# Expert blocks of 32 rows on four column groups, plain float32 weights in four whole buffers, loads begun while planning

## The chip, the cores and the metric

The kernel runs on one core of a Trainium2 chip. The metric is the device time of one launch in microseconds, the median of the timed runs. Everything is float32, and one launch does the whole of the computation below.

## What is computed

The reference is a trunk of two layers over 1,280 tokens of width 1,024 (256 context tokens and 1,024 latent tokens). Layer 0 mixes tokens by a convolution module, layer 1 by a gated linear attention. Each is followed by a mixture of experts. Layer 0's works on all 1,280 tokens, layer 1's on the 1,024 latent ones. The change concerns the mixture of experts alone:

```python
g_idx = argmax(h @ wg + bg)                      # one of 4 groups
inner = (h @ wr + br).reshape(t, 4, 8)[:, g_idx] # 8 experts in it
top_v, top_i = top_k(inner, 2)                   # two experts a token
top_w = softmax(top_v) * g_prob[g_idx]
expert = g_idx * 8 + top_i
# for each token's two experts e:
y = (silu(x @ w1[e]) * (x @ w3[e])) @ w2[e]      # w1, w3: 1024x512, w2: 512x1024
out[token] += top_w * y
```

Each layer has 32 experts with 6.29 MB of weights each. Layer 0 has 2,560 pairs of a token and an expert, layer 1 has 2,048. How many rows an expert gets depends on the data.

## The kernel before

The program is a row of stages; each is one block in which all engines run their own instruction streams, and a stage begins when all engines have finished the one ahead. In each layer the order around the experts is: `conv_out` or `gla_output` (which writes the normalised rows `hd` to memory and leaves the router's scores `lg` in a tile), `route`, `experts`, then `combine_values` or `combine`. `conv_taps` is an earlier stage of layer 0.

**`route`** plans. VectorE picks the two experts of each token, TensorE counts rows with two products (L1042, L1043), and VectorE works out each row's rank in its expert, in which block of rows it stands (`first`) and at which place in it (`mine`). From tables of places and blocks (`in_slot`, `in_blk`) TensorE makes the list of tokens of each block (L1048), `plan.token`. It also makes `plan.block`, the expert of each block, and `plan.fresh`, whether a block has another expert than the one ahead. VectorE waits for the constant tables at the start. The blocks are 128 rows long, and an expert takes as many as it needs; experts with no more than 128 rows take one.

**`experts`** runs one block after another. GpSimd gathers the block's 128 rows from `hd` into `xg` (L1317), after TensorE has turned the block ahead. TensorE turns them (`moe_pxt`, L1349), ScalarE and VectorE split them into a high part in float32r and the rest (`moe_xt_hi`, `moe_xt_lo`). The weights are split in the same way when a block is fresh: ScalarE copies each half matrix of 1 MB to `hi` (L1408) and VectorE subtracts it to get `lo` (L1479). Each product is three products, high by high, high by low and low by high:

```python
def product3(pe, out, xh, xl, wh, wl, start, stop):
    pe.matmul(out, xh, wh, start=start, stop=False)
    pe.matmul(out, xh, wl, start=False, stop=False)
    return pe.matmul(out, xl, wh, start=False, stop=stop)
```

In a block TensorE runs w1's and w3's products (24 matmuls of 512 columns each), turns the rows of the block behind it in order, runs w2's product of the block ahead (24 matmuls), and turns its own block's `a` = silu times product (`moe_pat`, L1388). ScalarE takes `py` out to `y` (L1418) and stores it (L1422). SyncE loads weights into `raw` (L1282): w1 and w3 have two raw buffers, w2 has one; a load waits until VectorE has made the low part of what stood there. At the end of layer 0 SyncE writes zeros over the blocks that are not used (L1302).

The bodies stand twice in a loop with a test whether the block is in the count. What is read from a table (`value_load`) sets which branch is taken.

## Time and profile before

| | |
|---|---|
| median of 3 runs | 3072.42 us |
| lowest, highest | 3071.2, 3075.68 us |
| the profiled execution's own time | 3072.33 us |
| its span, first to last instruction | 3070.6 us |
| mean granted clock of TensorE, share of full | 0.899 |
| TensorE busy (matmul / weight load) | 2519.3 / 2033.0 us |
| VectorE, ScalarE, GpSimd busy | 2006.1, 1432.9, 331.4 us |
| moved by DMA | 689 MB, 224 GB/s over the span |

Busy times of TensorE are lengths of pipelined instructions; two can overlap, so how densely they follow is read from their starts. In a row, `output<-inputs` names the tiles, and what stands in square brackets is the engine's idle time ahead of the group with what ended it. The rows on which the prediction rests stand in a section of their own below.

### The profile page before, as it was taken

The page shows a single profiled execution, that of the slowest core. Times are in us where ns is not written, and L with a number is a line of the kernel's source. Part 1 is how long each engine was busy: PE and PEld are TensorE (multiplying, and loading weights), DVE is VectorE, ACT ScalarE, POOL GpSimd, SP SyncE. Part 2 cuts the span into 40 slices and gives each one's busy share as a digit, 9 for nine tenths or more (in the row PEclk, how much of TensorE's full clock was granted, in tenths as well). Part 3 has the DMA queues.
Part 4 walks back from the last instruction along what each step waited for, and adds up shares of the span by engine and source line. Part 5 has one row for each costly group of instructions (what it writes and reads, how often), then busy time and mean ns, then how long its engine had stood idle before and what let it go on. Part 6 is the DMA issues. An engine that isn't in the chain of part 4 may idle for free. (4 is left out here: it accounts for less than half of the span.)

```text
span 3070.6 us, 40694 instructions
## 1 busy us (share of the span) xinstructions
PE 2519.3 (82%) x13249; PEld 2033.0 (66%) x13249; DVE 2006.1 (65%) x1989; ACT 1432.9 (47%) x1596; POOL 331.4 (11%) x381
## 2 busy tenths in 40 slices
PE   4488773695799999999948998979693999999970
PEld 0467662584588888888836876768583788888850
DVE  1559999665657786588526402347565788888855
ACT  0311001452546676577424313458331777777742
POOL 0000000100001000100012100043100100010004
PEclk8589887797799999999978999989796999999985
DMA  9354341221878899799655411025551999999956
GB/s 306 119 166 140 127 159 70 99 103 65 291 261 306 323 331 357 264 360 389 247 182 202 143 52 46 14 78 171 205 191 61 375 389 385 389 388 394 394 211 227
DMA packets 294341, 689.13 MB, mean 224 GB/s; under 512 B 22764, under 2 KB 49588, under 8 KB 294222
## 3 DMA queue, kind: packets, MB, share of 16 engines
q1 hardware_dynamic: 263058, 584.81, 52.8%
q0 software_dynamic: 17472, 56.72, 5.6%
q10 hardware_dynamic: 13712, 46.30, 4.0%
q8 instruction: 61, 1.00, 0.1%
q14 instruction: 38, 0.31, 0.0%
HBM read 597.74 MB, written 91.06 MB: 224 GB/s over the span
## 5 line engine op out<-in xcount | busy, mean ns | idle before, releaser
L1479 DVE TENSOR_TENSOR moe_w_lo<-moe_w_raw,moe_w_hi 128x2048 fp32r<-128x2048 f32 x384 | 861.8, 2285 | 81.8 <-ACT moe_w_hi L1408 48.0
L1408 ACT ACTIVATE moe_w_hi<-moe_w_raw 128x2048 fp32r<-128x2048 f32 x384 | 713.8, 1908 | 59.1 <-issue 38.3
L99 PE MATMUL moe_pg<-moe_w_hi,moe_xt_hi 128*128 128x512 f32 x592 | 243.4, 411 | 11.3 <-DVE moe_xt_lo L1490 5.9
L99 PE MATMUL moe_py<-moe_w_hi,moe_at_hi 128*128 128x512 f32 x592 | 242.0, 409 | 11.9 <-DVE moe_w_lo L1479 8.2
L100 PE MATMUL moe_pg<-moe_w_lo,moe_xt_hi 128*128 128x512 f32 x592 | 236.6, 400 | 0.0
L101 PE MATMUL moe_pg<-moe_w_hi,moe_xt_lo 128*128 128x512 f32 x592 | 236.1, 399 | 0.0
L100 PE MATMUL moe_py<-moe_w_lo,moe_at_hi 128*128 128x512 f32 x592 | 235.4, 398 | 0.0
L101 PE MATMUL moe_py<-moe_w_hi,moe_at_lo 128*128 128x512 f32 x592 | 235.3, 397 | 0.0
L101 PE MATMUL moe_pu<-moe_w_hi,moe_xt_lo 128*128 128x512 f32 x592 | 234.3, 396 | 0.0
L99 PE MATMUL moe_pu<-moe_w_hi,moe_xt_hi 128*128 128x512 f32 x592 | 234.1, 396 | 0.0
L100 PE MATMUL moe_pu<-moe_w_lo,moe_xt_hi 128*128 128x512 f32 x592 | 234.1, 396 | 0.0
L1525 DVE TENSOR_TENSOR moe_a<-moe_sil,moe_pu 128x512 f32<-128x512 f32 x74 | 50.9, 688 | 182.0 <-issue 133.2
L531 ACT ACTIVATE taps_sg<-taps_zg,channel_vectors 128x512 f32<-128x512 f32 (+1 forms) x24 | 14.8, 616 | 285.5 <-PE taps_za L101 285.5
L1418 ACT ACTIVATE moe_y<-moe_py 128x1024 f32<-128x1024 f32 x74 | 76.0, 1027 | 148.8 <-PE moe_py L101 148.8
L1433 ACT ACTIVATE moe_xt_hi<-moe_pxt 128x1024 fp32r<-128x1024 f32 x74 | 75.8, 1025 | 134.5 <-PE moe_pxt L1349 134.5
L99 PEld LDWEIGHTS moe_pg<-moe_w_hi,moe_xt_hi 128*128 128x128 f32 x592 | 113.1, 191 | 36.2 <-issue 12.4
L99 PEld LDWEIGHTS moe_py<-moe_w_hi,moe_at_hi 128*128 128x128 f32 x592 | 112.4, 190 | 35.9 <-issue 12.3
L1311 POOL COPY moe_idx<-plan_token 128x1 int32 (+1 forms) x76 | 16.0, 210 | 1077.1 <-PE moe_pxt L1349 1076.9
L101 PEld LDWEIGHTS moe_pg<-moe_w_hi,moe_xt_lo 128*128 128x128 f32 x592 | 113.0, 191 | 27.4
L101 PEld LDWEIGHTS moe_py<-moe_w_hi,moe_at_lo 128*128 128x128 f32 x592 | 112.2, 190 | 27.1
L99 PE MATMUL cv_acc<-cv_w_hi,ht_next_hi 128*128 128x512 f32 x288 | 116.9, 406 | 14.8 <-DVE ht_next_lo L2038 14.8
L99 PEld LDWEIGHTS moe_pu<-moe_w_hi,moe_xt_hi 128*128 128x128 f32 x592 | 111.2, 188 | 26.9
(348 smaller groups left out, 5397.5 us busy)
## 6 DMA issues: line engine op xcount, KB each, us to landing
moe_w_raw<-in_moe_w SPq DMA_DIRECT2D x384, 1024.0 KB, 12.7
taps_ada_w<-in_ada_w SPq DMA_DIRECT2D x40, 1024.0 KB, 6.9
scratch_experts_out<-moe_y ACTq DMA_DIRECT2D x57, 512.0 KB, 6.4
taps_raw<-in_conv_pw_w SPq DMA_DIRECT2D x20, 512.0 KB, 8.6
scan_v<-scratch_gla_values SPq DMA_DIRECT2D x20, 512.0 KB, 3.6
ada_w<-in_ada_w SPq DMA_DIRECT2D x4, 2048.0 KB, 29.8
cv_raw<-in_gla_w_in SPq DMA_DIRECT2D x16, 512.0 KB, 4.8
scratch_gla_out<-scan_o SPq DMA_DIRECT2D x16, 512.0 KB, 6.4
```

Source lines behind the costliest of these rows:

```text
L99: pe.matmul(out, xh, wh, start=start, stop=False)
L100: pe.matmul(out, xh, wl, start=False, stop=False)
L101: return pe.matmul(out, xl, wh, start=False, stop=stop)
L531: act.activation(sg[g][:, 0:m], zg[g][:, 0:m], ACT.Sigmoid, bias=vecs[:, n, V_BG:V_BG + 1])\
L1311: pool.tensor_copy(idx[:, :], plan.token[:, ds(k, 1)]).then_inc(s("idx_ready"), 1)
L1408: act.activation(hi[m][:, cut, :], raw[m][p][:, cut, :], ACT.Copy).then_inc(s(f"{m}_hi{h}"), 1)
L1418: act.activation(y[:, :], py[:, :], ACT.Copy).then_inc(s("y_out"), 1)
L1433: act.activation(xt_hi[:, :, :], pxt[:, :, :], ACT.Copy).then_inc(s("xt_hi"), 1)
L1479: dve.tensor_tensor(lo[m][:, cut, :], raw[m][p][:, cut, :], hi[m][:, cut, :].bitcast(F32), ALU.subtract).then_inc(s(f"{m}_lo{h}"), 1)
L1525: dve.tensor_tensor(a[:, :], sil[:, :], pu[:, :], ALU.mult).then_inc(s("a_ready"), 1)
```

## The change

- **Blocks are 32 rows.** `route` plans blocks of 32, in a fixed order of the experts (`EXPERT_ORDER`: expert 0 of each group, then expert 1 of each, and so on); each expert has at least one block. `plan.ends` says after which block each expert ends. `plan.fresh`, `plan.taken` and the table behind them go.
- **Four column groups.** In a product of 32 rows the output has 32 partitions. Four of them stand side by side: for w1 and w3 together each strip of 32 partitions takes 128 of the 512 hidden columns of both matrices, for w2 each strip takes 256 of the 1,024 output columns. All tiles of the stage shrink accordingly. A row of `hd` is gathered as four pieces of 256 values, to the four strips.
- **Plain float32.** Weights and rows are not split; each product is one float32 product.
- **Four whole buffers.** `Feed` holds four experts' weights (w1, w3, w2), 6.29 MB each. The loads of expert x + 3 start when expert x - 1 is done. The order is fixed, so SyncE needs no table to know which expert comes.
- **Loads begun while planning.** SyncE issues the loads of three experts in `route`; the planner's own tiles lie in the fourth buffer.
- **The loops.** TensorE goes by experts: the code of one block stands four times with tests, once in a loop for blocks 5 to 16 and once in a loop for more, for each of the four buffers, and that once ahead of the loop over experts and once in it. The other engines go by blocks, four bodies in a loop. GpSimd gathers four blocks ahead.
- **Around it.** The zeros are written in `conv_taps` by one DMA of 4 MB on ScalarE's queue. The planner's first constant (`ranks`) is loaded in the stage ahead. The token list product is cut into four strips.

```diff
-GROUPS, PER_GROUP, EXPERTS, FF, BLK = 4, 8, 32, 512, 128
+GROUPS, PER_GROUP, EXPERTS, FF, BLK = 4, 8, 32, 512, 32
+EXPERT_ORDER = [g * PER_GROUP + e for e in range(PER_GROUP) for g in range(GROUPS)]
+AHEAD_X = 4
+ROUND = float(1 << 23)
...
+                        if g == 2 and n == 1:
+                            act.wait_ge(s("zeros_set"), 1)
+                            act.dma_start(d.yd[2 * TOK:, :].rearrange("(p r) (s n) -> p (r s) n", p=P, n=D // 4),
+                                          zeros[:, :].unsqueeze(1).to_broadcast([P, EXPERTS * BLK // P * 4, D // 4]))\
+                                .then_inc(s("covered"), 16)
                         for at in units_behind(n, g):
...
+    PAIR = 2 * KC * FF
+    WORDS = PAIR + FF // P * D
...
+    def load_pair(self, sp, x):
+        e, b = EXPERT_ORDER[x], x % self.BUFS
+        for m, src in enumerate((self.d.w1, self.d.w3)):
+            for h in range(2):
+                sp.dma_start(self.pair[:, b, m, h * KC // 2:(h + 1) * KC // 2, :].rearrange("p (s c) n -> p s (c n)", c=2),
+                             src[self.layer, e, h * D // 2:(h + 1) * D // 2, :].rearrange("(s p c) n -> p s (c n)", p=P, c=2))\
+                    .then_inc(self.sem(f"pair_loaded{b}"), 16)
+    def load_back(self, sp, x):
+        e, b = EXPERT_ORDER[x], x % self.BUFS
+        for h in range(2):
+            sp.dma_start(self.back[:, b, 2 * h:2 * h + 2, :],
+                         self.d.w2[self.layer, e, h * FF // 2:(h + 1) * FF // 2, :].rearrange("(k p) n -> p k n", p=P))\
+                .then_inc(self.sem(f"back_loaded{b}"), 16)
...
+                for x in range(feed.AHEAD):
+                    feed.load_pair(sp, x)
+                    feed.load_back(sp, x)
...
-                pe.wait_ge(s("hot_slots"), 4)
                 for j in range(2 * nt):
-                    last = pe.matmul(pi[:, :], in_slot[:, j, :], in_blk[:, j, :], start=j == 0, stop=j == 2 * nt - 1)
+                    if j % nt == 0:
+                        pe.wait_ge(s("hot_slots"), 2 * (j // nt + 1))
+                    for r in range(0, P, BLK):
+                        last = pe.matmul(pi[r:r + BLK, :], in_slot[:, j, :], in_blk[:, j, :],
+                                         start=j == 0, stop=j == 2 * nt - 1)
                 last.then_inc(s("slots_done"), 1)
...
+                for x in range(feed.AHEAD, BUFS):
+                    feed.load_pair(sp, x)
+                    feed.load_back(sp, x)
+                for x in range(EXPERTS):
+                    times = x // BUFS + 1
+                    sp.wait_ge(feed.sem(f"pair_loaded{x % BUFS}"), 64 * times)
+                    sp.sem_inc(s("pair_ready"), 1)
+                    sp.wait_ge(feed.sem(f"back_loaded{x % BUFS}"), 32 * times)
+                    sp.sem_inc(s("back_ready"), 1)
+                    if 1 <= x < EXPERTS - feed.AHEAD:
+                        done = sp.value_load(plan.ends[0:1, x - 1:x], min_val=1, max_val=nb)
+                        sp.wait_ge(s("pair_done"), done)
+                        feed.load_pair(sp, x + feed.AHEAD)
+                        sp.wait_ge(s("back_done"), done)
+                        feed.load_back(sp, x + feed.AHEAD)
...
+                def gather(k, p):
+                    pool.tensor_copy(idx[:, p:p + 1], plan.token[:, ds(k, 1)]).then_inc(s("idx_ready"), 1)
+                    pool.wait_ge(s("idx_ready"), k + 1)
                     pool.sem_inc(s("gathers"), 1)
...
+                def out_product(out, buf):
+                    for c in range(STRIPS):
+                        for j in range(STRIPS):
+                            last = pe.matmul(out[j * BLK:(j + 1) * BLK, 0:CUT], at[:, c * BLK:(c + 1) * BLK],
+                                             feed.back[:, buf, c, j * CUT:(j + 1) * CUT], start=c == 0, stop=c == STRIPS - 1)
+                    last.then_inc(s("back_done"), 1)
+                def rows_of(k, x, b, nth):
+                    pe.wait_ge(s("xt_ready"), k + 1)
+                    if nth == 0:
+                        pe.wait_ge(s("pair_ready"), x + 1)
+                    for c in range(KC):
+                        for j in range(STRIPS):
+                            last = pe.matmul(pg[j * BLK:(j + 1) * BLK, 0:2 * P].rearrange("t (m n) -> t m n", m=2),
+                                             xt[:, c % 2, (c // 2) * BLK:(c // 2 + 1) * BLK],
+                                             feed.pair[:, b, :, c, j * P:(j + 1) * P], start=c == 0, stop=c == KC - 1)
+                    last.then_inc(s("pair_done"), 1)
+                    turn_x(k + 1)
+                    if started(k, 1):
+                        pe.wait_ge(s("at_ready"), k)
+                        if nth < 2:
+                            pe.wait_ge(s("back_ready"), x + nth)
+                        pe.wait_ge(s("y_out"), k)
+                        out_product(py, (b - 1) % BUFS if nth == 0 else b)
+                    pe.wait_ge(s("a_ready"), k + 1)
+                    pe.transpose(pat[:, 0:P], a[:, :], ident[:, :]).then_inc(s("at_turned"), 1)
+                def expert(x, b):
+                    first = 0 if isinstance(x, int) and x == 0 else \
+                        pe.value_load(plan.ends[0:1, ds(x - 1, 1)], min_val=1, max_val=nb)
+                    end = pe.value_load(plan.ends[0:1, ds(x, 1)], min_val=1, max_val=nb)
+                    rows_of(first, x, b, 0)
+                    for r in range(1, SOME):
+                        with pe.If(first + r < end):
+                            rows_of(first + r, x, b, r)
+                    with pe.If(first + SOME < end):
+                        with pe.Fori(SOME, MANY) as r:
+                            with pe.If(first + r < end):
+                                rows_of(first + r, x, b, SOME)
+                        with pe.If(first + MANY < end):
+                            with pe.Fori(MANY, (nb - EXPERTS) // 2) as r:
+                                with pe.If(first + r < end):
+                                    rows_of(first + r, x, b, SOME)
+                SOME, MANY = 4, 16
                 pe.wait_ge(s("ident"), 16)
-                turn_x(1)
-                blocks(pe, body, lambda count, last: out_product(count, last, 1))
+                turn_x(0)
+                for b in range(BUFS):
+                    expert(b, b)
+                with pe.Fori(1, EXPERTS // BUFS) as i:
+                    for b in range(BUFS):
+                        expert(i * BUFS + b, b)
+                count = pe.value_load(plan.block[0:1, 0:1], min_val=plan.fewest, max_val=nb)
+                pe.wait_ge(s("at_ready"), count)
+                pe.wait_ge(s("back_ready"), EXPERTS)
+                out_product(py_last, (EXPERTS - 1) % BUFS)
             @block.scalar
...
+                def take_x(k):
+                    act.wait_ge(s("xt_turned"), k + 1)
+                    act.activation(xt[:, :, :], pxt[:, 0:2 * P].rearrange("p (c n) -> p c n", c=2), ACT.Copy)\
+                        .then_inc(s("xt_ready"), 1)
+                def store(k, src, stored):
+                    act.dma_start(d.yd[ds(k * BLK, BLK), :].rearrange("t (s n) -> s t n", n=CUT), src).then_inc(s(stored), 16)
+                def body(k, i, p):
+                    act.wait_ge(s("pair_done"), k + 1)
+                    if started(k, 1):
+                        act.wait_ge(s("a_ready"), k)
+                    act.activation(sil[:, :], pg[:, 0:P], ACT.Silu).then_inc(s("sil_ready"), 1)
+                    take_x(k + 1)
+                    if started(k, 1):
+                        b = (p - 1) % UNROLL
+                        act.wait_ge(s("back_done"), k)
+                        if started(k, UNROLL + 1):
+                            act.wait_ge(s(f"y_stored{b}"), (i - (1 if p == 0 else 0)) * 16)
+                        act.activation(y[b][:, :], py[:, 0:CUT], ACT.Copy).then_inc(s("y_out"), 1)
+                        act.wait_ge(s("y_out"), k + 1)
...
+                def bring_x(k, i, p):
+                    dve.wait_ge(s(f"gathered{p}"), (i + 1) * 16)
+                    if started(k, 1):
+                        dve.wait_ge(s("xt_turned"), k)
+                    dve.tensor_copy(x_rows[:, :], xg[p][:, :]).then_inc(s("x_here"), 1)
+                def body(k, i, p):
+                    bring_x(k + 1, i + (p + 1) // UNROLL, (p + 1) % UNROLL)
+                    dve.wait_ge(s("sil_ready"), k + 1)
+                    if started(k, 1):
+                        dve.wait_ge(s("at_turned"), k)
+                    dve.tensor_tensor(a[:, :], sil[:, :], pg[:, P:2 * P], ALU.mult).then_inc(s("a_ready"), 1)
+                    dve.wait_ge(s("at_turned"), k + 1)
+                    dve.tensor_copy(at[:, :], pat[:, 0:P]).then_inc(s("at_ready"), 1)
```

## Rows read from the trace of the kernel before

**Rows 1.** The page, the span in 40 equal slices.
```profile
PE   4488773695799999999948998979693999999970
...
GB/s 306 119 166 140 127 159 70 99 103 65 291 261 306 323 331 357 264 360 389 247 182 202 143 52 46 14 78 171 205 191 61 375 389 385 389 388 394 394 211 227
```

**Rows 2.** Stage table: window, length, busy (count) by engine, granted clock, DMA share, GB/s.
```profile
726.00:781.00 55.00, 17.15 (x71) 15.03 (x70) 35.58 (x90) 3.82 (x8) 0.01 (x1) 0.51 0.06 23
781.00:1579.00 798.00, 767.90 (x3536) 624.76 (x3536) 529.69 (x318) 487.50 (x361) 72.98 (x88) 0.98 0.84 306
...
2330.00:2368.00 38.00, 9.11 (x36) 8.07 (x36) 28.79 (x83) 1.85 (x4) 0.13 (x1) 0.50 0.02 6
2368.00:2991.00 623.00, 587.97 (x2696) 478.07 (x2696) 506.03 (x288) 451.65 (x321) 61.95 (x68) 0.97 0.98 363
...
2500.00:2900.00 400.00, 400.00 (x1858) 325.97 (x1858) 349.33 (x200) 311.37 (x222) 39.33 (x44) 1.00 1.04 389
```

**Rows 3.** Stage table of tile moe_sil alone: VectorE, ScalarE.
```profile
781.00:1579.00 798.00, 28.87 (x42) 24.42 (x42) 0.98 0.84 306
2368.00:2991.00 623.00, 22.02 (x32) 18.52 (x32) 0.97 0.98 363
```

**Rows 4.** Timeline of TensorE in one block: start, length, instruction, count.
```profile
961.78 0.48 PE L99 MATMUL moe_pg<-moe_w_hi,moe_xt_hi 128*128 128x512 f32 x1
...
973.06 1.03 PE L1349 MATMUL moe_pxt<-moe_ident,moe_xg 128*128 128x128 f32 x8
...
979.52 0.60 PE L1388 MATMUL moe_pat<-moe_ident,moe_a 128*128 128x128 f32 x4
```

**Rows 5.** Timeline at a modulation group; that tile's instruction row.
```profile
167.61 0.39 PE L101 MATMUL taps_za<-ht_conv_hi,taps_w_lo 128*128 128x512 f32 x1
167.93 0.40 PE L481 MATMUL taps_ada_acc<-taps_ada_b,taps_one 1*2 1x128 f32 x8
168.25 1.93 PE L488 MATMUL taps_ada_acc<-taps_ada_w,silu_c 128*2 128x128 f32 x64
...
L488 PE MATMUL taps_ada_acc<-taps_ada_w,silu_c x1280: 271/273/421, 168.3 to 486.0; 128*2 128x128 f32 x183
```

**Rows 6.** Timeline of TensorE in the scan; one tile's instruction row.
```profile
2065.84 1.89 PE L2434 MATMUL scan_po<-scan_state,scan_qs 128*128 128x256 f32 x8
2067.57 1.89 PE L2443 MATMUL scan_pds<-scan_v,scan_kst 128*128 128x256 f32 x8
...
2089.49 1.15 PE L2394 MATMUL scan_patt<-scan_qi,scan_ki 128*64 128x64 f32 x32
...
L2394 PE MATMUL scan_patt<-scan_qi,scan_ki x256: 222/222/270, 2047.4 to 2147.3; 128*64 128x64 f32 x128
```

**Rows 7.** Timeline from the planner's start to the first expert product, layer 0.
```profile
741.31 0.20 DVE L1071 TENSOR_REDUCE route_gm<-scores 128x10 f32<-128x40 f32 x1 [4.44 <-DMA route_next_e<-const_next_expert]
...
770.80 8.78 PE L1048 MATMUL route_pi<-route_in_blk,route_in_slot 128*128 128x53 f32 x40 [18.08 <-DVE route_in_blk L1148]
...
783.52 713.42 SPq L1282 DMA_DIRECT2D moe_w_raw<-in_moe_w  x192
...
797.52 0.77 PE L99 MATMUL moe_pg<-moe_w_hi,moe_xt_hi 128*128 128x512 f32 x1 [2.69 <-issue]
```

**Rows 8.** Timeline: ScalarE after a branch; TensorE after a gap and when faster.
```profile
823.95 3.72 ACT L1408 ACTIVATE moe_w_hi<-moe_w_raw 128x2048 fp32r<-128x2048 f32 x2 [0.45 <-issue]
...
815.50 0.61 PE L99 MATMUL moe_pg<-moe_w_hi,moe_xt_hi 128*128 128x512 f32 x1 [3.00 <-DVE moe_xt_lo L1490]
...
819.22 0.39 PE L99 MATMUL moe_pg<-moe_w_hi,moe_xt_hi 128*128 128x512 f32 x1
```

**Rows 9.** The page: a queue's packets and bytes; a DMA's median to landing.
```profile
q8 instruction: 61, 1.00, 0.1%
...
moe_xg<-scratch_experts_in,moe_idx POOLq DMA_INDIRECT x76, 7.6
```

**Rows 10.** Timeline: the last store of layer 0's experts.
```profile
1571.48 0.34 ACTq L1422 DMA_DIRECT2D scratch_experts_out<-moe_y  x1
```

More of the change, by code:

```diff
@@ L1019, in route @@
-        more = ph.sb("more", [P, 2 * nt * nt + EXPERTS * nt])
-        need = ph.sb("need", [P, EXPERTS])
-        ends = [ph.sb(f"ends{j}", [P, EXPERTS]) for j in range(2)]
-        passed = ph.sb("passed", [1, nb, EXPERTS])
-        blk = ph.sb("blk", [1, nb + 2])
-        fresh = ph.sb("fresh", [1, nb])
-        in_slot = ph.sb("in_slot", [P, 2 * nt, P])
-        in_blk = ph.sb("in_blk", [P, 2 * nt, nb + 1])
+        sb = feed.room()
+        before = sb([P, P])
+        ones = sb([P, P])
+        iota = sb([P, P])
@@ new lines, in route @@
+        token = sb([P, TILES])
+        strip = sb([P, 1])
+        gm = sb([P, nt])
+        ga = sb([P, nt, GROUPS])
+        gsel = sb([P, nt, GROUPS])
+        gw = sb([P, nt])
+        inner = [sb([P, nt, EXPERTS]) for j in range(2)]
+        cand = sb([P, nt, EXPERTS])
+        least = sb([P, nt])
+        top = sb([P, 2, nt])
+        hot = sb([P, 2, nt, EXPERTS])
+        both = sb([P, nt, EXPERTS])
+        sofar = sb([P, nt + 1, EXPERTS])
+        rank = sb([P, nt, EXPERTS])
+        picked = sb([P, 2, nt, EXPERTS])
@@ L1027, in route @@
+        mine = sb([P, 2, nt])
+        first = sb([P, 2, nt])
+        over = sb([P, 2, nt])
+        need = sb([P, EXPERTS])
+        ends = [sb([P, EXPERTS]) for j in range(2)]
+        in_slot = sb([P, 2 * nt, BLK])
+        in_blk = sb([P, 2 * nt, nb + AHEAD_X])
         pr = ph.ps("pr", [P, nt * EXPERTS])
         pa = ph.ps("pa", [P, nt * EXPERTS])
-        pi = ph.ps("pi", [P, nb + 1])
+        pi = ph.ps("pi", [P, nb + AHEAD_X])
         with nc.Block() as block:
@@ L1130, in _ @@
-                link(dve.tensor_reduce(first[:, :, :], picked[:, :, :, :], AX.X, ALU.add))
-                for j in range(2):
-                    full = more[:, j * nt * nt:j * nt * nt + nt * (nt - 1)].rearrange("p (t k) -> p t k", k=nt - 1)
-                    link(dve.tensor_tensor(full, over_rows(mine[:, j, :], nt - 1),
-                                           steps[:, 1:nt].unsqueeze(1).to_broadcast([P, nt, nt - 1]), ALU.is_ge))
-                    link(dve.tensor_reduce(over[:, j, :], full, AX.X, ALU.add))
@@ L1213, in experts @@
[L1213 to L1227 removed]
+        ident = ph.sb("ident", [P, P])
+        idx = ph.sb("idx", [P, UNROLL], I32)
@@ L1228, in blocks @@
+        cut_rows = d.hd.rearrange("t (s n) -> (t s) n", n=CUT)
+        def blocks(eng, body, tail=None):
+            count = eng.value_load(plan.block[0:1, 0:1], min_val=plan.fewest, max_val=nb)
+            for k in range(UNROLL):
+                body(k, 0, k)
+            with eng.Fori(1, nb // UNROLL) as i:
+                for p in range(UNROLL):
+                    k = i * UNROLL + p
                     with eng.If(k < count):
-                        body(k, 2, i, p)
-                    if otherwise:
-                        with eng.If(k >= count):
-                            otherwise(k)
+                        body(k, i, p)
@@ L1530, in experts @@
+                bring_x(0, 0, 0)
+                blocks(dve, body)
+        ph.sems.update(feed.sems)
         ph.close()
```

480 lines of the change are left out of this document (154 added, 326 removed).

## The prediction

> **What bounds the kernel now.** I read the slices first, to see which engine fills which part. TensorE is at 9 tenths in the parts where the weight traffic is also high [rows 1]. The table by stage then gives two expert stages, 781 to 1579 us and 2368 to 2991 us, with 55 and 38 us of planning ahead of them [rows 2]. The count of silu instructions says how many blocks of 128 rows each has: 42 and 32 [rows 3]. In a block 48 matmuls of 512 columns start in 11.28 us, 0.235 each, and a block takes 17.74 + 0.36 = 18.1 us [rows 4]. 42 x 18.1 = 760 of the 798 us: layer 0 is bound by TensorE, with DMA at 0.84. In layer 1 both are full: 32 x 18.1 = 579 of 623 us, while the stretch 2500 to 2900 moves 389 GB/s at a DMA share of 1.04 [rows 2]. An expert's weights are 6.29 MB. All 32 must be brought in either kernel, so layer 1 can gain little but its idle DMA during planning (0.02 share [rows 2]).
>
> **How many blocks of 32.** The reference's router on its own inputs gives each expert's rows. Cut in 128s they make 42 and 32 blocks, as the trace has. Cut in 32s they make 96 and 79, in the fixed order: layer 0 1 2 1 12 1 1 1 8 3 1 1 6 1 2 1 8 2 1 1 11 4 1 1 2 1 1 1 3 1 1 1 14; layer 1 one to four each, mostly 2 or 3, the last 4.
>
> **Removed.** The splits into high and low parts (384 ScalarE and as many VectorE instructions) and two of three products. ScalarE and VectorE were beside TensorE in both stages (487 and 530 of 798 us [rows 2]), so their end is worth nothing by itself.
>
> **A block on TensorE, T.** Plain float32 runs as two instructions a product. Eight of 256 columns take 1.89 us with the last one's run-out; the next group follows within 1.73, 0.216 each [rows 6], so 213 ns of columns at the granted 2.4 GHz. The pair product is 8 x 4 products, 64 instructions; the second is 4 x 4, 32 instructions. One after the other that is 96 x 0.213 = 20.4 us. Whether four column groups really run side by side decides everything, and before already does it for the modulation: 64 instructions of 128 columns, four strips in turn, take 1.93 us [rows 5]. Alone each needs 107 ns, 6.8 us together; (1.93 - 0.27)/63 = 26 ns is a quarter. So 64 x 53 = 3.4 us and 32 x 53 = 1.7 us.
> In that row the stationary side has 2 columns, here 32. The nearest row with a wider one has 64 in two groups: 32 starts in (1.15 - 0.22)/31 = 30 ns where 26.7 would be full overlap, 0.89 of it [rows 6]. It has as many loads per column time as could ever hurt here, so it is the upper bound: 5.1/0.89 = 5.75 us.
> The Trainium skill (TensorE: Matmul & The Clock Gate, Part 3: Packing small matmuls) gives 2.38 times for three column tiles, 0.79 of full overlap; by that T would be near 7.5 us and the kernel slower. The row of 64 instructions contradicts it for a long stream; I let the row decide and keep the rule as a rival.
> Three transposes at 0.1 us add 0.3 [rows 4]. The array changes between four strips and whole four times a block. A change from whole to strips costs 0.32 instead of 0.225 us between starts [rows 5], 0.1; one back also waits for the last instruction of a strip, 0.16 more. 2 x 0.1 + 2 x 0.26 = 0.7. T = 3.4 + 1.7 + 0.3 + 0.7 = 6.1, taken as 6.2 us; ends 5.4 (changes free) and 6.85 (0.89 overlap).
> The rest hides behind it. Silu and product of 128x128 tiles are under 0.3 us each and lie behind the next transposes and the second product (2.3 us). ScalarE's copy, silu, output copy and store issue come to about 1.5 us a block, GpSimd's index copy and gather issue to 2 to 3 us; the gather runs four blocks (25 us) ahead of a 7.6 us landing [rows 9].
>
> **Per expert, E.** TensorE's queue reads two entries of the table and branches up to six times. ScalarE's reading and branching in before shows 0.45 us [rows 8]; some of it runs ahead of the array. I take 1 us, ends 0 and 4.5 (rivals). After a gap of 3 us the array restarted at a start spacing of 0.43 us and was at full rate 3.7 us later [rows 8]; I charge 2.5 us to an expert that follows such a gap. The Trainium skill (TensorEngine Tiling (Array Packing), Key Properties) says that changing the mode drains the array, which is the 0.1 and 0.26 us above.
>
> **Loads, W.** Rows are read in pieces of 4 KB instead of 2 (first two matrices). 395 GB/s, a little above the 389, makes 15.9 us an expert; ends 366 (some slices of the expert stages show 357 to 369 [rows 1]) and 408 GB/s, 17.2 and 15.4. A block of 32 rows gathers and stores 0.26 MB in 1 KB pieces: 0.8 us of DMA; 1.3 if such pieces run at half rate.
>
> **Planning.** VectorE no longer waits for its tables, 4.4 us [rows 7] less the 1 us of the stage's change. Removed ops are the 7 us behind the last table, hidden under TensorE's 8.8 us [rows 7]; that product becomes 160 instructions in four strips, half of them behind the other table, 4 us exposed at the low clock. Narrower tables and fewer steps save 1.4 us. So stage two begins 8 us earlier, near 773 and 2360. First loads start at 741 and 2333 instead of 783.5 and 2370.7; three experts (48 us) fit. The first block needs a gather (7 us), one copy, two transposes, one copy: TensorE starts at 784 (before 797.5 [rows 7]) and 2369. The ten zero stores at the end of layer 0 become one 4 MB store on ScalarE's queue during the tap stage: 10 to 16 us of DMA at a stage with a low share, its issue between two sigmoids. I charge 2 us, ends 0 and 12 if ScalarE's queue is held. The small `ranks` loads cost nothing: SyncE has finished its stage's loads.
>
> **The sum.** One rule for each layer: weights of an expert land W + 0.8n after the later of the previous landing and the end of the expert four before; TensorE starts it when both it and the weights are free and takes 6.2n + 1. Layer 0: landings 758, 775, 792; the 12-block expert runs 818 to 895, the 11-block one 1147 to 1216; in the heavy stretches all four buffers are full and DMA stands, in the light ones TensorE waits. The last, 14 blocks, lands at 1388 with TensorE free at 1370: the order puts the largest last. It ends at 1478. After it the last output, its store and the stage's close take 10 us (before 7.5 us behind the store's issue [rows 10]): 1488, 91 us earlier than 1579. Layer 1: DMA sets the pace, 79 x 6.2 + 32 = 522 us of TensorE against 573 of DMA; last landing 2906, last expert 2910 to 2936, end 2946, 45 us earlier. From the profiled execution's 3072.3 us (span 3070.6; median of the runs 3072.4, so no shift): 3072.3 - 91 - 45 + 2 = **2938 us**.
>
> The same rule with one term changed: T 5.4 gives 2893, 6.85 gives 3004, 7.3 gives 3064; E 0 gives 2925, 2 gives 2962, 3 gives 2992, 4.5 gives 3073, 7 gives 3210; W 15.4 gives 2917, 17.2 gives 3001; 1.3 us a block for small pieces 3009.
>
> **Rivals.**
> 1. Code (other side). TensorE's program for an expert is six copies of one block's code, about 1,200 instructions, written out for eight experts. Before's whole program came over the instruction queue in 61 packets, 1.00 MB [rows 9], for 26,498 TensorE instructions executed, so its loop stayed resident. Here a one-block expert jumps over five copies, one of 2 or 3 blocks over three or four. If each jump must wait for code, a wait costs from less than 1 us up to a gather's landing, 7.6 us [rows 9], less some 2 us that the queue runs ahead. It decides from E = 4.5 us on: E 5 gives 3100, E 7 gives 3210. For it: no row shows such long jumps. Against: forward jumps go the way code is fetched. The Trainium skill (Runtime: NRT & Kernel Launch, Instruction fetch mechanics) says that a taken branch beyond the window forces a DMA fetch; no row here shows one. Chance 0.17.
> 2. Overlap worse than in the row (wide stationary side, different moving data in each strip, T 7.5): 7.5 and 1 give 3095. Against it stands [rows 5]. 0.07.
> 3. Strips one after another, T = 21: 5400 us, the change then doesn't do what it says. 0.02.
> 4. The array stays at 1.2 GHz, products double, T 11.3: 3720. The array waits for weights in the light stretches, yet with two stationary columns it came to full rate in before. 0.03.
> 5. Pieces of 1 KB and 366 GB/s at once, DMA-bound: 3089. 0.04.
> 6. Control and mode changes dearer but below break-even (T 6.9 or E 2.5 to 4): 2990 to 3065. 0.17.
> 7. Everything at its good end (T 5.4, W 15.4): near 2859 to 2890. 0.07.
>
> The forecast with its own range 2890 to 2990 has 0.43. Against no change I can tell 0.2%, 6 us, from none. Faster: 0.43 + 0.07 + 0.17 + a little of the rest = 0.69; same 0.04; slower 0.27. Range: case 7's 2870 to 3115, which takes in case 5, half of 1 and most of 2.
>
> **What would show it.** Right: 64 pair instructions in 3.4 to 3.8 us, four strips started 53 ns apart; 6.2 us from one silu to the next within the 12- and 14-block experts; weight loads in the planning windows; DMA share near 1 through layer 1; TensorE waiting for pair loads there; some 17 us of waiting ahead of the last expert of layer 0. Wrong: starts 200 ns apart; gaps of 3 us or more ahead of each expert's first block with its weights landed, and many more packets on the instruction queue; a clock of 0.5 in the heavy stretches; or VectorE, ScalarE or GpSimd named as releaser ahead of most blocks.

## The result and the profile after

The changed kernel takes **3709.6 us** (median of 4 runs, 3706.2 to 3710.9) against 3071.8 us for the one before: ratio 1.207, 95% interval 1.205 to 1.209. I had forecast 2938 us and a range up to 3115. It is 638 us slower.

The page of the changed kernel: its slices (as [rows 1]), the instruction queue (as [rows 9]), and the costliest group of instructions with its idle time and what ended that.

```profile
PE   4587728837575568544939989769455546555580
...
GB/s 276 127 211 137 148 82 92 94 369 152 270 165 235 247 165 166 271 250 154 36 189 168 76 41 12 150 196 188 285 274 244 233 224 230 249 228 229 228 35 194
...
q8 instruction: 392, 6.42, 0.8%
...
L1364 PE MATMUL moe_pg<-feed_w,moe_xt 128*32 128x256 f32 x11200 | 778.4, 437 | 771.0 <-issue 770.0
```

The table by stage, columns as in [rows 2]: planning and experts of layer 0, then of layer 1. The windows run from SyncE's first issue in one stage to its first issue in the next.

```profile
737.00:774.00 37.00, 8.92 (x164) 7.37 (x164) 24.29 (x78) 1.73 (x3) 0.00 (x0) 0.59 0.94 366
774.00:1871.00 1097.00, 664.52 (x9506) 353.15 (x9506) 84.06 (x289) 102.09 (x290) 116.39 (x200) 0.78 0.53 197
2622.00:2659.00 37.00, 6.53 (x132) 5.44 (x132) 21.14 (x76) 1.72 (x3) 0.00 (x0) 0.55 0.94 366
2659.00:3624.00 965.00, 556.96 (x7823) 289.50 (x7823) 69.23 (x238) 84.31 (x239) 96.64 (x166) 0.78 0.59 220
```

TensorE's timeline in layer 0, first the second expert (two blocks) and the start of the third (one block), then a block in the middle of the 12-block expert; the number in brackets is the gap ahead.

```profile
815.01 5.22 PE L1364 MATMUL moe_pg<-feed_w,moe_xt 128*32 128x256 f32 x64 [15.16 <-issue]
...
822.72 3.66 PE L1364 MATMUL moe_pg<-feed_w,moe_xt 128*32 128x256 f32 x64
...
842.99 6.58 PE L1364 MATMUL moe_pg<-feed_w,moe_xt 128*32 128x256 f32 x64 [14.05 <-issue]
...
877.18 3.66 PE L1364 MATMUL moe_pg<-feed_w,moe_xt 128*32 128x256 f32 x64
880.77 0.50 PE L1346 MATMUL moe_pxt<-moe_ident,moe_x_rows 128*128 128x128 f32 x2
881.20 1.93 PE L1352 MATMUL moe_py<-feed_w,moe_at 128*32 128x256 f32 x32
883.07 0.33 PE L1377 MATMUL moe_pat<-moe_ident,moe_a 128*128 128x128 f32 x1
883.33 3.66 PE L1364 MATMUL moe_pg<-feed_w,moe_xt 128*32 128x256 f32 x64
```

What to see. The expert stages grew from 798 and 623 us [rows 2] to 1097 and 965. Planning ends earlier in layer 0 (774 against 781), but in layer 1 it takes 37 us, as it did before the change. Inside the 12-block expert a block takes 883.33 - 877.18 = 6.15 us: the four column groups do run side by side (64 instructions in 3.66 us). But DMA stands at 0.53 and 0.59, so weights aren't short. Ahead of most experts (47 of 62) TensorE is idle for 11 to 17 us, and the profile calls that "issue": time in which the engine waits for nothing that the profile shows, no semaphore and no data. It is 770 us in 67 gaps, 765 of them in the 62 gaps between experts. The instruction queue, which brings the engines' code, carried 392 packets of 16.4 KB (6.42 MB) where it had 61 [rows 9]. After a gap the pair product (w1's and w3's together) takes 5.0 to 6.7 us in place of 3.66 (two with a further gap inside take longer). Over all 175 blocks slow starts cost another 778.4 - 175 x 3.66 = 138 us.

### The profile page after: what moved, and what is told of

Same layout as the page of the kernel before. It is cut to its first block and busy times, and to the rows that moved or that the text cites. A ratio compares the mean times of both kernels' runs of the same rounds, so it can differ in the third digit from the quotient of the medians.

```text
span 3704.4 us, 61196 instructions
## 1 busy us (share of the span) xinstructions
PE 2379.8 (64%) x24562; PEld 1567.6 (42%) x24563; DVE 1108.9 (30%) x1895; ACT 680.3 (18%) x1442; POOL 410.4 (11%) x591
## 3 DMA queue, kind: packets, MB, share of 16 engines
q8 instruction: 392, 6.42, 0.8%
## 5 line engine op out<-in xcount | busy, mean ns | idle before, releaser
L1364 PE MATMUL moe_pg<-feed_w,moe_xt 128*32 128x256 f32 x11200 | 778.4, 437 | 771.0 <-issue 770.0
L1364 PEld LDWEIGHTS moe_pg<-feed_w,moe_xt 128*32 128x32 f32 x11200 | 398.8, 125 | 1092.4 <-issue 916.4
L1352 PE MATMUL moe_py<-feed_w,moe_at 128*32 128x256 f32 x5536 | 334.6, 382 | 0.0
L1352 PEld LDWEIGHTS moe_py<-feed_w,moe_at 128*32 128x32 f32 x5536 | 161.6, 109 | 110.6
L1323 POOL DMA_INDIRECT moe_xg<-scratch_experts_in,moe_idx x183 | 179.3, 980 | 144.4 <-POOL moe_idx L1320 143.3
L1346 PE MATMUL moe_pxt<-moe_ident,moe_x_rows 128*128 128x128 f32 x354 | 89.4, 334 | 50.4 <-DMA moe_ident<-const_ident 50.4
L104 PE MATMUL cv_acc<-cv_w_hi,ht_next_lo 128*128 128x512 f32 x288 | 115.3, 400 | 0.0
L103 PE MATMUL cv_acc<-cv_w_lo,ht_next_hi 128*128 128x512 f32 x288 | 114.9, 399 | 0.0
L600 DVE SCALAR_TENSOR_TENSOR taps_acc<-taps_back,channel_vectors,taps_acc 128x649 f32<-128x649 f32 x120 | 107.0, 891 | 0.0
L588 DVE SCALAR_TENSOR_TENSOR taps_acc<-taps_u,taps_both,taps_acc 128x649 f32<-128x649 f32 x120 | 106.9, 891 | 0.0
L615 DVE SCALAR_TENSOR_TENSOR taps_acc<-taps_ahead,channel_vectors,taps_acc 128x649 f32<-128x649 f32 x112 | 92.0, 891 | 0.0
```

The lines of the kernel that those rows point to most:

```text
L588: dve.scalar_tensor_tensor(acc[0][:, :], src, tap, acc[0][:, :], ALU.mult, ALU.add)\
L600: dve.scalar_tensor_tensor(acc[1][:, :], src, tap, acc[1][:, :], ALU.mult, ALU.add)\
L615: dve.scalar_tensor_tensor(acc[q][:, :], src, tap, acc[q][:, :], ALU.mult, ALU.add)\
L1323: pool.indirect_dma_start(xg[p][:, :], None, cut_rows, bass.IndirectOffsetOnAxis(idx[:, p:p + 1], 0))\
L1346: last = pe.transpose(pxt[:, c * P:(c + 1) * P], x_rows[:, c::2], ident[:, :])
L1352: last = pe.matmul(out[j * BLK:(j + 1) * BLK, 0:CUT], at[:, c * BLK:(c + 1) * BLK], feed.back[:, buf, c, j * CUT:(j + 1) * CUT], start=c = ...
```

## The experiments

**Theory A**: code. An expert has six written copies of the block's code, a copy 198 matmul and weight-load instructions, and an expert with few blocks steps over the unused ones from jump to jump; each lands in code that isn't at hand. **B**: the branches and table reads themselves. **C**: weights, or the queue that loads them. And: does the price of A depend on the weight traffic beside it?

e1, e5, e8, e9, e10 and e12 are medians of 4 to 9 runs; e2, e3, e4, e6, e7 and e11 are one run each. In all of them "gap" is the idle time of TensorE ahead of an expert's first pair product (L1364), and the sum of a kernel is the line "issue" of that group.

**e1: two copies**

```
-                SOME, MANY = 4, 16
+                SOME, MANY = 1, 16
-                        with pe.If(first + MANY < end):
-                            with pe.Fori(MANY, ...) as r: ...
```

> The expert code of TensorE is cut from six written copies of the block body per buffer (four in a row, two in loops) to two (the first block, and one in a loop up to 16 blocks; no expert of either layer has more). All arithmetic is the same. Theory A, code that is jumped over must be fetched: the loop over four buffers shrinks from about 24 copies to 8, about 1,700 instructions; if that stays at hand, the instruction queue falls from 392 packets to about 150 and the gap between experts from 12 to 17 us to under 2 us, expert stages 1087 and 970 us towards 700 and 540, in all 2880 to 3050 us. If only the skipped copies are saved but each pass still fetches its code, the gap falls to about 6 us and the time to 3250 to 3400 us. Rival B, the table reads and the branches themselves cost the gap: two reads per expert stay and one branch per block stays, the gap stays over 10 us and the time over 3550 us. Rival C, weights: nothing changes in the loads, the gap stays, 3700 us.

**e2: three copies** (`SOME = 2`, the second loop left out)

> Three written copies per buffer (first, second, loop up to 16). Theory A: the loop over four buffers is about 2,500 instructions and does not stay at hand if the limit lies between 1,700 and 2,500; each expert fetches its own three copies, about half of what six need, so the gap is about 7 us and the time about 3300 us; with everything at hand as in the two-copy kernel, 2900 to 3050. Rival B: more branches are taken than with two copies, so about as slow as the changed kernel, over 3550. Rival C: 3700.

**e3: five copies** (`SOME = 4`, the second loop left out)

> Five written copies per buffer: only the second loop (blocks 17 on, never run) is dropped from the changed kernel. Theory A, code fetched page after page as it is jumped over: one copy of about 13 KB less per expert, so 64 x 0.8 pages x 2.8 us = about 140 us less, 3560 us, and about 50 instruction packets fewer. If only what is entered is fetched, no change: 3700. Rivals B and C: 3700.

**e4: no weight traffic** (the changed kernel; from the fifth expert on each weight load is cut to 16 columns, w2's in the same way, so the products use old weights; layer 1's routing changes with the values, and only layer 0 is compared)

```
+        if x >= self.BUFS:
+            sp.dma_start(self.pair[:, b, m, h * KC // 2, 0:16], src[..., 0:16])...
+            continue
```

> The changed kernel with the weight loads of experts 5 to 32 of each layer cut to slices of 16 columns (so the products use old weights; the output is not the reference's). The weight traffic of some 350 MB goes, every wait on weights goes. Theory A with a fetch price of its own: the gaps between experts stay at 12 to 17 us, the time stays near 3700 us, within 60 us. Theory A with contention, code waits behind weights in the DMA engines: the gaps shrink to under 7 us and the time to under 3350 us. Rival C, the gap is a wait for weights or for the queue that loads them: gaps vanish, under 3000 us.

Measured: e1 3360.8 us (ratio to before 1.0945, 1.0926 to 1.0963), e2 3343.0, e3 3605.8, e4 3450.4. Instruction packets 83, 234, 337, 392; issue gaps 412, 422, 666, 532 us. The e1 page, and three rows of its timeline: the experts that follow one of 2, of 8 and of 3 blocks.

```profile
q8 instruction: 83, 1.36, 0.2%
```

```profile
822.36 5.56 PE L1364 MATMUL moe_pg<-feed_w,moe_xt 128*32 128x256 f32 x64 [10.54 <-issue]
...
1002.95 5.72 PE L1364 MATMUL moe_pg<-feed_w,moe_xt 128*32 128x256 f32 x64 [6.52 <-issue]
...
1033.22 5.94 PE L1364 MATMUL moe_pg<-feed_w,moe_xt 128*32 128x256 f32 x64 [9.70 <-issue]
```

With the code at hand (83 packets against 392) the issue gaps after a one-block expert of layer 0 fall from 13.1 us on average to 0.2 to 2.6. So A is there. But 412 us of issue are left where I had expected under 2 us an expert, and e1 misses its 2880 to 3050 us. Its time lies in the 3250 to 3400 that I gave to another case, each pass fetching its code; the packets refute that case. After 2, 3, 8 and 12 blocks the gap is 10.54, 9.70, 6.52, 3.38 us. It falls with each block that the expert has: the loop makes 15 trips whatever the expert needs, and an expert of 2 blocks makes 14 empty trips and one of 12 blocks makes 4, so a trip that only jumps over its body costs (10.54 - 3.38) / 10 = 0.72 us. That is B, in a place where I hadn't looked. In the changed kernel it is small (35 such trips ahead of another expert in layer 0, 25 us; none in layer 1). One copy less (e3) is worth 55 packets and 104 us, near the 140 that A gave. e2, with three copies, came out near the 3300 that A gave; its code is fetched again (234 packets), but it has fewer empty trips than e1. C is out: e4 without the traffic still has gaps. Yet they are shorter: in layer 0 they sum to 283 us against 396 in the changed kernel, with the same packets. So 0.29 of the wait goes when the weight traffic goes, and e4's time lies between the two answers that I had written down.

**e5: the loop ends at the expert's last block**

```
-                    with pe.If(first + SOME < end):
-                        with pe.Fori(SOME, MANY) as r:
-                            with pe.If(first + r < end):
-                                rows_of(first + r, x, b, SOME)
+                    with pe.If(first + 1 < end):
+                        with pe.Fori(1, end - first) as r:
+                            rows_of(first + r, x, b, 1)
```

> The two-copy kernel with the loop over the later blocks ending at the expert's own last block (its end read from the table), and not run at all for experts of one block, in place of 15 trips of which most jump over the body. In the two-copy kernel the gap after an expert of 2, 4, 8, 12 blocks is 10.5, 9.0, 6.6, 3.4 us, 0.68 us for each empty trip. Rival B (empty trips cost) takes all of these gaps away, down to about 1 us an expert: about 412 - 64 = 350 us less on TensorE, part of which the weight loads (15.9 us an expert) give back: 2870 to 3050 us. If the gap after the loop is instead the way back from a long loop to the next copy (a code matter, once per expert), it stays at 3 to 10 us: over 3250 us.

**e6: one unused copy; e7: four** (e5 and, behind the loop, `for r in range(1)` or `range(4)`: `with pe.If(first + 20 < end): rows_of(first + 20, x, b, 2)`, which no expert enters)

> The kernel above with one more written copy of the block body behind each expert's loop, jumped over by every expert (it is for a 21st block). Nothing else is done or left out. Theory A: the loop over four buffers no longer stays at hand (12 copies, about 2,500 instructions); the instruction queue rises from about 83 to about 230 packets, 2 to 3 an expert at 1 to 2.8 us each, and the time rises by 64 x 3 to 64 x 7 us less what weight waits hide: 100 to 350 us more. If code that is only jumped over costs nothing: within 20 us (one branch of 0.3 us an expert).

> The same with four unused copies, so six per buffer as in the changed kernel. Theory A: about 390 instruction packets and the gaps of the changed kernel (12 to 15 us after light experts); its time is that of the changed kernel less its own empty trips (37 trips of 0.68 us in layer 0, 25 us) or more: 3550 to 3690 us. If jumped-over code is free and only branches cost: 3 branches more than one copy, under 3100 us.

**e8: all loops to their ends** (e5 and `with eng.Fori(1, (count + UNROLL - 1) >> 2)` in `blocks`, for ScalarE, VectorE and GpSimd)

> As the first kernel of this call, and the loops of ScalarE, VectorE and GpSimd over blocks end at the last block too (they run 27 groups of four, of which 24 and 20 groups hold blocks). At the end of an expert stage ScalarE takes its last result 6.6 us (layer 0) after TensorE had it; in layer 1, with 33 trips over, TensorE's own records before its last product show 8.6 us of gap. Expect 10 to 25 us less than the kernel above if these trips end the stages; nothing (within 6 us) if the code behind them is what is late.

Measured: e5 3056.4 us (ratio 0.9949, 0.9936 to 0.9963), e6 3174.5, e7 3899.2, e8 3042.7 (0.9905, 0.9881 to 0.9930). Packets 137, 234, 385, 137. Who ended TensorE's waits ahead of the pair product, in e5, then in e7:

```profile
L1364 PE MATMUL moe_pg<-feed_w,moe_xt x11200: 376/379/637, 794.0 to 2952.8; 128*32 128x256 f32 x197
its engine sat idle before it (us, times) until:
  SPq L1305: 125.3, 22
  issue: 80.2, 34
```

```profile
L1364 PE MATMUL moe_pg<-feed_w,moe_xt x11200: 379/379/636, 793.0 to 3791.1; 128*32 128x256 f32 x197
its engine sat idle before it (us, times) until:
  issue: 959.6, 63
```

e6 and e7 are the proof for A: they do the work of e5, and code that nobody runs costs 118 and 843 us. The branches that come with it can't be the cause: with the code at hand a whole empty trip, its branch included, costs 0.72 us (e1), so four of them are under 3 us an expert. The first extra copy brings 97 packets, the next three 151 more at 4.5 us of issue each, (959.6 - 286.6) / 151; I had expected 1 to 2.8, and e7 lies far above its range of 3550 to 3690.

I had counted copies, but what sets the gap is rather the number of jumps in a row. The changed kernel steps over its last two copies with one branch (the second loop stands inside the first one's condition), so a one-block expert makes four jumps there and five in e7, over five copies in both. The gap behind a one-block expert of layer 0 is on average 4.9 us with one jump (e11, below), 5.7 and 5.8 with two (e2, e6), 11.2 and 13.1 with four (e3 and the changed kernel) and 16.0 with five (e7). Of these only e11 changes the jumps and keeps the copies. The trace of e7 shows the chain itself. In the gap from 800 to 819 us four packets come over the instruction queue:

```profile
q8 instruction: 4, 0.07, 1.4%
```

They start at 803.6, 809.5, 815.2 and 818.4 us and take 1.1 us each. So they come one at a time, each long after the one before is there. From one start to the next it is 5.9 and 5.7 us while weights load and 3.2 us once the weights have landed (the DMA share is under 0.4 from 816 us on). Over all of e7's gaps the median is 5.7 us where DMA is over 0.9 busy, and where it is under 0.1 the times are 3.1 to 5.2 us. One more place shows the chain: behind the 12-block expert, which steps over one copy in the changed kernel and over four in e7.

```profile
948.61 4.98 PE L1364 MATMUL moe_pg<-feed_w,moe_xt 128*32 128x256 f32 x64 [3.75 <-issue]
```

```profile
966.55 6.37 PE L1364 MATMUL moe_pg<-feed_w,moe_xt 128*32 128x256 f32 x64 [14.36 <-issue]
```

3.75 us contains four empty trips, 2.9 us by e1's price; with four copies, four jumps and no empty trip it is 14.36. e5 lies 6 us above its range of 2870 to 3050, since waits for weights (125 us, 45 in e1) took part of what the trips gave back. e8 gains 14 us on e5: the last result is taken right after TensorE's last product in place of 6.6 us later.

**e9: loop head on a page** (e8 and `head_slot={pe.engine: 0}` on TensorE's loop over four buffers)

> The kernel with all loops to their ends, and the head of TensorE's loop over four buffers put at the start of a page of 256 instructions. In that kernel layer 0 shows no such gap, but in layer 1 each of the seven trips begins with a gap of 9 to 12.5 us that the trace puts to issue, and the instruction queue took 54 packets more than in the two-copy kernel, about 8 a trip. Theory, the loop touches one page too many in layer 1 by where it happens to lie: 7 gaps of 10 us go, about 60 us less with some given back to weight waits: 2975 to 3010 us, and 85 to 90 instruction packets. If the gaps are something else in layer 1 (its loads, its plan), nothing changes: 3043 us and 137 packets.

**e10: hinted back edge** (e8 and `hint_back_edge=True` on the same loop)

> Same base, and in place of the placement a hint at the top of each trip of that loop, for the branch back to its head. If a hint brings only the head's page early, each of layer 1's trips still fetches the pages behind it, which follow in order while the first copy runs: the 10 us gap shrinks to a few us, 2990 to 3030 us, with packets still near 137. If the hint does nothing: 3043. If each hint disturbs pages at hand in layer 0: slower than 3043.

**e11: nested branches** (the changed kernel, its six copies kept)

```
-                    for r in range(1, SOME):
-                        with pe.If(first + r < end):
-                            rows_of(first + r, x, b, r)
+                    def later(r):
+                        with pe.If(first + r < end):
+                            if r < SOME:
+                                rows_of(first + r, x, b, r)
+                                later(r + 1)
+                            else:
+                                loops()
```

> The changed kernel with the same six copies and the same loops, but each later copy's branch nested in the one before, so an expert with few blocks jumps once over all that it does not use in place of stepping from copy to copy. Theory A with its price in the chain (each jump lands on a page that is not at hand, the next jump is only seen then): one or two fetches an expert in place of five, the instruction queue falls from 392 to 200 to 270 packets, the gaps from 12 to 16 us to 3 to 7 us, the time to 3150 to 3350 us. If the price is per expert and not per page (one stall whatever is skipped): 3650 to 3710.

Measured: e9 3043.5 us (ratio 0.9898, 0.9880 to 0.9916), e10 3039.6 (0.9885, 0.9867 to 0.9903), e11 3396.4. Packets 84, 83, 314. The 21st expert of layer 1 (the first of a trip of the loop over four buffers) in e8 and in e9; the SPq rows are waits for weights:

```profile
2708.35 5.93 PE L1364 MATMUL moe_pg<-feed_w,moe_xt 128*32 128x256 f32 x64 [10.03 <-issue]
```

```profile
2713.22 3.66 PE L1364 MATMUL moe_pg<-feed_w,moe_xt 128*32 128x256 f32 x64 [0.71 <-issue]
...
2730.28 5.78 PE L1364 MATMUL moe_pg<-feed_w,moe_xt 128*32 128x256 f32 x64 [4.69 <-SPq L1305]
...
2749.12 4.90 PE L1364 MATMUL moe_pg<-feed_w,moe_xt 128*32 128x256 f32 x64 [4.35 <-SPq L1305]
```

And the waits ahead of e9's pair products, then its stages by time (layer 0, layer 1, a stretch of layer 1):

```profile
L1364 PE MATMUL moe_pg<-feed_w,moe_xt x11200: 376/379/637, 790.8 to 2946.3; 128*32 128x256 f32 x197
its engine sat idle before it (us, times) until:
  SPq L1305: 176.7, 34
  issue: 15.4, 24
```

```profile
770.00:1530.00 760.00, 619.95 (x9506) 333.58 (x9506) 83.76 (x289) 101.88 (x290) 115.91 (x200) 0.91 0.73 283
2330.00:2960.00 630.00, 518.89 (x7823) 277.02 (x7823) 68.95 (x238) 82.83 (x238) 94.83 (x163) 0.91 0.90 331
2440.00:2860.00 420.00, 344.82 (x5123) 181.89 (x5119) 44.80 (x154) 53.88 (x155) 59.06 (x102) 0.90 0.99 355
```

The fetches of layer 1's trips were a matter of where the loop happens to lie: placed, it stays at hand (84 packets for 137), and the 10 us gaps go. The time doesn't move. 61 us of issue gave way to 50 us more of waiting for weights: behind the code stood the DMA engines, at 0.99. My 2975 to 3010 was wrong for the reason that this case teaches: a stall was costed without asking what is late next. e10 took away the same fetches, where I had expected packets near 137; e9 and e10 can't be told apart by their intervals. e11 shows what the chain of jumps costs: the same six copies, one jump in place of four, and 313 us less than the changed kernel with 78 packets fewer. It lies above its range of 3150 to 3350, with 314 packets where I had 200 to 270.

**e12: short gathers** (e9 and this edit; the products use partly old inputs, so again only layer 0 is compared)

```
-                    pool.indirect_dma_start(xg[p][:, :], None, cut_rows, ...)
+                    n = 16 if started(k, UNROLL) else CUT
+                    pool.indirect_dma_start(xg[p][:, 0:n], None, cut_rows, ...)
```

> The kernel with all loops to their ends and its loop head on a page, with each gather of a block's input, from the fifth block of a layer on, cut from 256 to 16 columns a row (the products use partly old inputs; the output is not the reference's). That kernel waits 177 us for weights: in layer 1 an expert takes 19.0 us, at a DMA share of 1.0 and 351 GB/s. Theory, traffic in 1 KB pieces beside the weights costs more than its bytes (I had 0.8 us a block): with half of it gone layer 1 goes to about 17.5 us an expert and 370 GB/s or more, the time to 2990 to 3015 us. Rival, the weights' own pieces set the rate: only the gathers' bytes go, 0.33 us a block, 32 to 35 us over both layers at most where weights bind, 3015 to 3035 us, with the weights' own rate unchanged. Rival, SyncE's issuing of six loads an expert (18 us) is the limit whatever is moved: 3043 us.

Measured: 3002.9 us (ratio 0.9759, 0.9739 to 0.9778). In layer 0 weight waits ahead of an expert fall from 94 to 84 us and the last store comes at 1505.8 in place of 1516.9 us, 11 us earlier. Layer 1 here has 80 blocks cut otherwise, so its share of the 41 us proves nothing about my theory, and the time inside the theory's range is no proof: the test is inconclusive there. What the traces do show is the rate of the weight queue, in e9 and then in e12, 2440 to 2860 us (packets, MB, share of the 16 engines):

```profile
q1 hardware_dynamic: 35252, 135.93, 89.2%
```

```profile
q1 hardware_dynamic: 36437, 140.46, 87.9%
```

Per engine time that is 135.93 / (0.892 x 420 us) = 363 GB/s beside whole gathers and 380 beside short ones, so the gathers seem to slow the weights' own packets by some 5%. Part of that may be that DMA was 0.94 busy in e12 and 0.99 in e9. The changed kernel moves more still where few blocks run beside the weights; its rate of DMA from 2500 to 2900 us in 40 slices:

```profile
GB/s 158 145 212 276 212 175 295 107 159 52 52 107 161 415 410 409 401 402 406 406 82 218 265 235 334 350 138 408 148 148 406 135 227 408 55 263 359 109 263 405
```

Planning and the first experts move 401 to 415 GB/s in full slices; with gathers and stores running e9 moves 355 (its last stage row above).

## Why the prediction was wrong

- **The step that failed is E, 1 us an expert, with rival 1 given 0.17.** Measured in the changed kernel: 395.5 us of gaps over 31 experts in layer 0, 12.8 each, and 369.2 over 31 in layer 1, 11.9 each. Reads and branches are as cheap as I said (e9, from the second trip of layer 0's loop on: 0.1 to 0.7 us an expert). The code is not: e1, e5 to e7 and e11 show it by packets and by time. The mechanism and its sign were in rival 1 in full. What was wrong was its price and its chance. I let "before's loop stayed resident" and "forward jumps go the way code is fetched" speak against it, and gave one wait per expert less than 1 to 7.6 us less a lead of 2 us. But waits come one behind the other, as e7's packets show (5.9, 5.7 and 3.2 us from one to the next). Its 3210 us for E 7 held half of the chain. And it left out a second price: my rule charges 2.5 us for the slow start behind a gap of 3 us, so from E = 3 on to every expert, and the list of results for other E doesn't. With that charge, and the counts of blocks that the traces show, the rule gives 3119 us for E 3, 3205 for E 4.5 and 3365 for E 7, so the break-even was near 3 us and not at 4.5. With the measured 12.3 us it gives 3705 against 3709.6 measured. So near a hit is in part luck, since the smaller terms below were off too; but the rule was sound, and E was the term that failed in it.
- The Trainium skill (Runtime: NRT & Kernel Launch, Instruction fetch mechanics) says that a taken branch out of the window forces a DMA fetch before execution goes on. The runs agree: 392 packets, and per packet above e9's 84 (770.0 - 15.4) / 308 = 2.45 us of issue, 1.9 in e11, 4.5 from e6 to e7. The same section of the Trainium skill gives TensorE room for 2,048 instructions: eight copies (about 1,600) stayed, twelve (about 2,400) did not (e6, 234 packets), which agrees. The same section of the Trainium skill says "The IRAM is only 2 cache lines" and gives a line 16 KiB; for TensorE that doesn't fit e9, whose loop of about 1,600 instructions ran with 84 packets in the whole program.
- **The slow start behind a gap** was 2.5 us in my rule, for a few experts. It is 1.3 to 3.1 us and came behind every one of the 62 gaps, 138 us in all; the granted clock is 0.78 over layer 0's experts, 0.91 in e9.
- **T = 6.2**: right, 6.15 us; rivals 2, 3, 4 and 7 are out. The 12-block expert keeps that pace from its second block on.
- **Planning 8 us earlier**: 6.6 us earlier in layer 0 (774.4 against 781.0) and nothing in layer 1, where planning takes 37.0 us against 37.3. (The 55 us for layer 0 in [rows 2] begin 12 us ahead of the stage, whose first issue by SyncE comes at 737.9 us.) VectorE did finish early, but a stage ends with its last engine, and that is now SyncE, which sits in the issues of the third expert's loads:

```profile
2649.54 0.27 DVE L1225 TENSOR_SCALAR plan_token<-feed_w 128x100 int32<-128x100 f32 x1
...
2653.64 4.91 SPq L1030 DMA_DIRECT2D feed_w<-in_moe_w  x2
2659.42 1.52 SPq L1298 DMA_DIRECT2D moe_ident<-const_ident  x1
...
2676.84 0.70 PE L1346 MATMUL moe_pxt<-moe_ident,moe_x_rows 128*128 128x128 f32 x2 [27.78 <-DMA moe_ident<-const_ident]
```

  The last row is the second thing that I did not follow on that queue: `moe_ident` is loaded by SyncE behind the weight loads now and lands 17 us into the stage. So the first product came at 792.6 us, not 784. 50.4 us of TensorE's idle time end with that load in the changed kernel and 49.1 in e9 (much of that lies under planning). In layer 1 of e9 the first product is 18.6 us behind the start of the stage (2327.2 to 2345.8), where I had 9.
- **Loads**: W was too low, the 0.8 us a block was right. With the code at hand (e9) layer 1's weights come between 2292.7 and 2908.2 us, 19.2 us an expert, not 15.9 + 2.5 x 0.8 = 17.9. At 363 GB/s of engine time an expert's 6.29 MB are 17.3 us. Gathers and stores have 9.3% of the 420 us for 51 blocks, 0.77 us a block. Rival 5, with 17.2 + 2.5 x 1.3 = 20.4 us, had the slower weights right and the small pieces wrong. My list has 3001 us for W 17.2, so this is about 63 of the 105 us between 2938 and e9's 3043. The rest is layer 1's planning, the late first products and slow starts; no run splits it further.

So of the miss of 772 us, 666 are code with its slow starts and empty loop trips, 14 of them those of the other engines (changed kernel to e9; part of what they free goes to weight waits), and about 105 the rest. The design does beat the kernel before once its code fits, by 1.0 to 1.2% (e9, e10), which is less than the 4.4% of my forecast.

## What to carry to other kernels

Count the code of each engine's loop, not only its instructions executed: written copies times buffers, against what stays at hand (here eight copies of 198, not twelve). A branch over code that isn't there costs a fetch, and branches in a row cost their fetches in a row; so nest them, let loops end at the true count, and watch the instruction queue's packets. When a rival's sign and place are known and no row shows its price, price it at its worst before giving it a small chance: here the waits come in a row, and each stall also brings a slow start. When a stall is to go, work out the next bound before promising its length. And when loads move into an earlier stage, ask what else their queue carries and whether the engine that issues them now ends that stage.

## What the runs showed of the hardware

- A loop of TensorE of about 1,600 matmul and weight-load instructions (eight copies) stays at hand; where it starts decides at the margin: 137 packets (e8) or 84 (e9) for the same code. A hint on the branch back did the same (e10, 83).
- A trip of a loop that only jumps over its body costs 0.7 us on TensorE even with the code at hand (e1).
- A packet of code of 16.4 KB takes 1.1 us itself. In a chain of jumps the next one starts 5.7 us (median) after the one before where DMA is over 0.9 busy, 3.1 to 5.2 us where it is under 0.1 (e7). Per packet above e9's 84 the issue time is 1.8 us in e6; from e6 to e7 it is 4.5 us a packet. Without weight loads the waits of layer 0 are 0.29 shorter (e4, 283 against 396 us).
- Gathers and stores in 1 KB pieces took 9.3% of the DMA engines for 31.7 GB/s in e9, some 6% more a byte than the weights (89.2% for 324 GB/s); beside them the weights ran at 363 GB/s of engine time, beside short gathers at 380 (e12).
